# A Hyena layer's filters made beside the product in front of it, and its convolutions laid among its input panels

## The reference

```python
def hyena_mixer(h, w_in, short_w, short_b, f_w1, ..., f_skip, w_out):
    v, x1, x2 = jnp.split(depthwise_conv3(h @ w_in, short_w, short_b), 3, axis=-1)
    h_freq = hyena_filters(seq, f_w1, f_b1, f_w2, f_b2, f_w3, f_freq)   # hid @ w3, decayed, / sum |h|, rfft
    def long_conv(u, n):
        uf = u.astype(jnp.float32)
        y = jnp.fft.irfft(jnp.fft.rfft(uf, n=2 * seq, axis=1) * h_freq[:, n], n=2 * seq, axis=1)[:, :seq]
        return (y + uf * f_skip[n].astype(jnp.float32)).astype(u.dtype)
    z = x1 * long_conv(v, 0)
    z = x2 * long_conv(z, 1)
    return z @ w_out
```

## Time and profile before

| | |
|---|---|
| median of 3 runs | 1804.94 us |
| profiled execution, its own time | 1802.81 us |
| its span | 1801.0 us |
| TensorE busy | 1740.6 us (97%) |
| VectorE busy | 1230.6 us (68%) |
| ScalarE busy | 985.2 us (55%) |

### The profile page before, as it was taken

How to read it: one execution, slowest core, us unless ns; L and a number is a source line. 1 busy time by engine, 2 the same in 40 slices (tenths; PEclk the granted TensorE clock), 3 DMA queues, 4 the chain that set the end, 5 groups by cost and what they waited for, 6 DMA issues and landing times.

```text
span 1801.0 us, 37562 instructions
## 1 busy us (share of the span) xinstructions
PE 1740.6 (97%) x13784; PEld 1646.0 (91%) x13784; DVE 1230.6 (68%) x2017; ACT 985.2 (55%) x1368; POOL 12.8 (1%) x20
## 2 busy tenths in 40 slices
PE   7999999999999998999999999999999999999997
PEld 7999999888999987569999999999999777799997
DVE  6887666586666587888666678766566656576654
ACT  4467744365775444216774446775454644467742
POOL 0000200000000000000000000000000000000000
PEclk9999999999999999999999999999999999999999
DMA  6567564433656453205666456656455332256661
GB/s 208 170 197 228 185 219 141 150 105 106 198 183 217 157 198 127 82 1 156 194 184 217 138 175 178 197 186 236 158 174 152 127 132 69 71 174 188 185 214 67
DMA packets 79400, 290.13 MB, mean 161 GB/s; under 512 B 9723, under 2 KB 12124, under 8 KB 79196
## 3 DMA queue, kind: packets, MB, share of 16 engines
q1 hardware_dynamic: 79324, 289.12, 50.6%
HBM read 288.03 MB, written 1.05 MB: 161 GB/s over the span
## 4 chain that ended last, share of the span: by engine, by line
PE 86%; DVE 9%; issue 2%; ACT 2%; DMA 1%; DVEq 0%; SPq 0%; ACTq 0%
PE bank L490 24%; PE bank L492 24%; PE bank L491 24%; DVE wlo L1440 2%; PE bank L802 2%; PE bank L781 1%; PE bank L721 1%; DVE conv_cv L1548 1%; DVE rinv L1446 1%; PE bank L865 1%; PE bank L963 1%; PE bank L700 1%; PE bank L973 0%; DMA raw<-in_w 0%; PE bank L936 0%
## 5 line engine op out<-in xcount | busy, mean ns | idle before, releaser
L490 PE MATMUL bank<-xh,whi 128*128 128x256 f32 (+1 forms) x2736 | 775.5, 283 | 11.0 <-DVE wlo L1440 10.6
L491 PE MATMUL bank<-xl,whi 128*128 128x256 f32 (+1 forms) x2736 | 772.1, 282 | 0.0
L492 PE MATMUL bank<-xh,wlo 128*128 128x256 f32 (+1 forms) x2736 | 771.4, 282 | 0.0
L1060 ACT CAST whi<-raw 128x1024 fp32r<-128x1024 f32 (+1 forms) x490 | 538.3, 1099 | 367.6 <-PE bank L492 322.6
L1440 DVE TENSOR_TENSOR wlo<-raw,whi 128x1024 fp32r<-128x1024 f32 (+1 forms) x491 | 629.1, 1281 | 4.8 <-ACT whi L1060 2.7
L490 PEld LDWEIGHTS bank<-xh,whi 128*128 128x128 f32 x2736 | 518.6, 190 | 26.8 <-issue 15.3
L492 PEld LDWEIGHTS bank<-xh,wlo 128*128 128x128 f32 x2736 | 519.2, 190 | 0.0
L491 PEld LDWEIGHTS bank<-xl,whi 128*128 128x128 f32 x2736 | 515.9, 189 | 0.1
L490 PE MATMUL bank<-ffn_hh,whi 128*128 128x256 f32 x880 | 246.7, 280 | 0.0
L492 PE MATMUL bank<-ffn_hh,wlo 128*128 128x256 f32 x880 | 246.7, 280 | 0.0
L491 PE MATMUL bank<-ffn_hl,whi 128*128 128x256 f32 x880 | 245.7, 279 | 0.0
(11 more groups left out here) (323 smaller groups left out, 2034.2 us busy)
## 6 DMA issues: line engine op xcount, KB each, us to landing
raw<-in_w SPq DMA_DIRECT2D x414, 512.0 KB, 3.6
raw<-in_w SPq DMA_DIRECT2D x80, 704.0 KB, 4.2
att_bias<-in_bias SPq DMA_DIRECT2D x4, 512.0 KB, 5.3
hy_w<-in_filt_w SPq DMA_DIRECT2D x8, 256.0 KB, 4.3
hy_decay<-in_decay SPq DMA_DIRECT2D x4, 512.0 KB, 5.2
mla_uq<-in_uq SPq DMA_DIRECT2D x1, 1152.0 KB, 5.2
x<-in_xT SPq DMA_DIRECT2D x1, 1024.0 KB, 5.8
out<-x SPq DMA_DIRECT2D x8, 128.0 KB, 2.0
```

The source lines that it names most:

```text
L490: pe.matmul(ps, whi[:, slot, wc], hi[:, k, cols], start=first, stop=False)
L491: pe.matmul(ps, whi[:, slot, wc], lo[:, k, cols], start=False, stop=False)
L492: mm = pe.matmul(ps, wlo[:, slot, wc], hi[:, k, cols], start=False, stop=last)
L1060: nc.scalar.copy(whi[:, p % RING, 0:k * P], raw[:, p % RING, 0:k * P]).then_inc(panel_hi, 1)
```

## The change

- The filter sets 0 and 1 are made beside the 16 panels of `down1`, the product in front of the Hyena layer (`first_filters`, one list of steps per engine, called after each panel). Their tables are loaded among the panels of `up1`, to buffers laid behind the feed-forward's.
- The 24 panels of `in2` are written out one by one; from panel 8 on they take turns in two banks, 0 and 1. Filter sets 2 and 3 use banks 2 and 3, the convolutions banks 4 to 7.
- Units 0, 1 and 2 are laid among the panels, one per six panels: TensorE does `turn` after panel 5+6u, `spectra` after 6+6u and 7+6u, `back` after 9+6u and 10+6u; VectorE does `multiply` behind its steps for panels 7+6u and 8+6u, `unit_out` behind 10+6u and 11+6u. Unit 3 stays behind the panels, with the rest of set 3.
- The skip terms are made by ScalarE (`skip`), not by VectorE. The copy that mended the first row of the magnitudes is replaced by a memset before the maximum.
- The key's rotation moves behind gate panel 12; the first sigmoid moves behind the first query of the latent attention.

The diff, cut to what the text speaks of:

```diff
-    hyx = overlay("hyx", [("ab", [P, 2, 2, HC], F32), ("ut", [P, 2, HC], F32), ("am", [P, 2, HC], F32)])
+    hyx = overlay("hyx", [("ut", [P, 2, HC], F32)])
+    skipped = [up[:, 0, 0:SEQ], up[:, 1, 0:SEQ], square[:, 0, 0:SEQ], square[:, 1, 0:SEQ]]
+    def in2_bank(p):
+        return (IN2.b0 + (p if p < 8 else p % 2)) % 4
 # SP
+            elif name == "up1":
+                panels(ph, 0, 8)
+                sp.wait_ge(y_lo, YBASE["in1"] + C)
+                sp.dma_start(hy["hdft"][:], a["hdft"]).then_inc(hs["tables"], 16)
+                panels(ph, 8, 4)
+                filter_inputs(0)
+                panels(ph, 12, 4)
+                sp.dma_start(hy["idft"][:], a["idft"]).then_inc(hs["tables"], 16)
...
+            elif name == "down1":
+                panels(ph, 0, 9)
+                more_filter_inputs(1)
+                panels(ph, 9, 7)
             elif name == "in2":
-                panels(ph, 0, 8)
-                sp.wait_ge(panel_used, ph.p0)
-                sp.dma_start(hy["fdft"][:], a["fdft"]).then_inc(hs["tables"], 16)
...
-                filter_inputs(0)
-                panels(ph, 8, 16)
+                panels(ph, 0, 3)
+                more_filter_inputs(2)
+                panels(ph, 3, 16)
+                more_filter_inputs(3)
+                panels(ph, 19, 5)
 # TensorE, beside down1
+        def first_filters(p):
+            if p in (0, 7):
+                for r in range(2):
+                    filters(p // 7, r)
+            elif p in (4, 11):
+                pe.wait_ge(hs["tables"], 64)
+                filter_sums(p // 7)
+                filter_spectra(p // 7, range(3))
+            elif p in (5, 12):
+                filter_spectra(p // 7, range(3, 5))
 # TensorE, in2
+            for p in range(2, 24):
+                if p < 8:
+                    panel(ph, 0, p, xh, xl, A, None)
+                else:
+                    panel(ph, 0, p, xh, xl, A, None, (in2_bank(p), ph.t0 + p + (1 if p < 10 else 3)))
+                u, at_ = divmod(p - 5, 6)
+                if p == 14:
+                    filter_sums(2)
+                    filter_spectra(2, (0,))
+                elif p == 15:
+                    filter_spectra(2, (1, 2))
+                elif p == 17:
+                    filter_spectra(2, (3, 4))
+                if 0 <= u < 3:
+                    if at_ == 0:
+                        turn(u)
+                    elif at_ in (1, 2):
+                        spectra(u, at_ - 1)
+                    elif at_ in (4, 5):
+                        back(u, (2 * at_ - 8, 2 * at_ - 7))
+                if p in (8, 10):
+                    filters(2, (p - 8) // 2)
+                elif p in (19, 21):
+                    filters(3, (p - 19) // 2)
+            turn(3)
+            filter_sums(3)
+            filter_spectra(3, (0,))
+            spectra(3, 0)
+            filter_spectra(3, (1, 2))
+            spectra(3, 1)
+            filter_spectra(3, (3, 4))
+            out_slices(range(0, HJ))
+            back(3, range(HJ))
             out_slices(range(HJ, C))
 # TensorE: what the new steps wait for
+            def turn(u):
...
+                if u < 2:
+                    pe.wait_ge(hs["zin"], HJ * (u + 1))
+                if u:
+                    pe.wait_ge(hs["z"], HJ * (u - 1) + 2)
...
+            def back(u, js):
+                pe.wait_ge(hs["Y"], 2 * u + 2)
 # ScalarE
+            def skip(u):
...
+                for j in range(HJ):
+                    cc = HJ * (u % 2) + j
+                    e = nc.scalar.activation(skipped[j], hy["z"][:, cc, :], ACT.Identity, bias=0.0,
+                                             scale=v("c_skip", u // 2 * C + cc))
+                e.then_inc(hs["skip"], 1)
+            for p in range(24):
+                tap(0, p, K8)
+                if p in (5, 11, 17, 23):
...
+                    turned((p - 5) // 6)
+                if p in (8, 14, 20):
...
+                    skip((p - 8) // 6)
...
 # VectorE, in2
+            for p in range(24):
+                conv_step(p)
+                u, at_ = divmod(p - 7, 6)
+                if p == 6:
+                    wing_weights(2)
+                elif p == 9:
+                    decayed(2, 0)
+                elif p == 11:
+                    decayed(2, 1)
+                elif p == 13:
+                    filter_magnitudes(2)
+                elif p == 14:
+                    inverse_sum(2)
+                elif p == 16:
+                    wing(2, 0)
+                if 0 <= u < 3:
+                    if at_ in (0, 1):
+                        multiply(u, at_)
+                    elif at_ == 3:
+                        unit_out(u, (0, 1))
+                    elif at_ == 4 and u < 2:
+                        unit_out(u, (2, 3))
...
+                elif p == 23:
+                    filter_magnitudes(3)
+                    unit_out(2, (2, 3))
+            inverse_sum(3)
+            wing(3, 0)
+            wing(3, 1)
+            multiply(3, 0)
+            multiply(3, 1)
+            unit_out(3, range(HJ))
-                if g == 2:
-                    key_rope()
...
             gate_tile(12)
+            key_rope()
             gate_tile(13)
```

More of the change, by code:

```diff
@@ L683, in attention @@
                 panel(PH["out1"], j // 4, j % 4, at["yh"], at["yl"], A, None)
-        def hyena(norm):
[L686 to L722, removed]
-            def turn(u):
[L726 to L729, removed]
@@ new lines, in filters @@
+        def filters(n, r):
+            pe.wait_ge(hs["ws"], n + 1)
+            if r and n >= 2:
+                pe.wait_ge(hs["ab"], 2 * n + 1)
+            elif n == 2:
+                pe.wait_ge(bank_free, IN2.t0 + 12)
+            elif n and not r:
+                pe.wait_ge(hs["wings"], n)
+                pe.wait_ge(hs["middle"], n)
+                pe.wait_ge(hs["inv"], n)
+            for part in range(2):
+                rows = slice(FHID * part, FHID * part + FHID)
+                mm = pe.matmul(filter_bank(n, part, r)[:], filt_hid[rows, r * P:(r + 1) * P], pair[rows, :],
+                               start=True, stop=True)
+            mm.then_inc(hs["F"], 1)
@@ L736, in out_slices @@
+            def back(u, js):
+                pe.wait_ge(hs["Y"], 2 * u + 2)
+                for j in js:
+                    for i in range(4):
+                        mm = pe.matmul(bank[4 + j][:, 0:SEQ], hy["frY"][:, i, j * P:(j + 1) * P], hy["idft"][:, i, :],
+                                       start=i == 0, stop=i == 3)
+                    mm.then_inc(hs["back"], 1)
             def out_slices(ks):
@@ L752, in out_slices @@
                             mm.then_inc(panel_used, 1)
-            ph = PH["in2"]
+            ph = IN2
             first_panels(ph, xh, xl, A, (x_lo, C * norm), norm, A)
[L756 to L791, removed]
-                else:
[L793 to L804, removed]
@@ L1007, in _ @@
             norm += 1
-            product(f"down{layer}", ffn["hh"], ffn["hl"], A, (hid_lo, FC * layer))
+            if layer == 1:
+                for p in range(16):
+                    panel(PH["down1"], p // 4, p % 4, ffn["hh"], ffn["hl"], A, (hid_lo, FC))
+                    first_filters(p)
+            else:
+                product(f"down{layer}", ffn["hh"], ffn["hl"], A, (hid_lo, FC * layer))
         retention_in(norm)
@@ L1085, in step @@
                 split_hi(ph, 0, i, j, k)
-            steps(act, ph, 0, ph.n, step, loop=gain is not None)
+            if between is None:
+                steps(act, ph, 0, ph.n, step, loop=gain is not None)
+            else:
+                for p in range(ph.n):
+                    step(p // 4, p % 4, ph.k if p + 4 < ph.n else ph.next_k)
+                    between(p)
         def conv_tap(name, m):
@@ L1481, in step @@
                                     square[:, (j // 2 if half else j) % 2, next_cols], ALU.add).then_inc(sum_added, 1)
-            dve_steps(ph, 0, ph.n, step)
+            if between is None:
+                dve_steps(ph, 0, ph.n, step)
+            else:
+                for p in range(ph.n):
+                    step(p // 4, p % 4, ph.k if p + 3 < ph.n else ph.next_k)
+                    between(p)
         def scaled(ph, first, n, dst, keep=None):
```

380 lines of the change are left out of this document (215 added, 165 removed).

## The result

The changed kernel took 1820.16 us in the median of 4 runs (1816.5 to 1824.04), the kernel before 1804.93 beside it (1802.77 to 1805.02): a ratio of 1.0085, 95% interval 1.007 to 1.01. It is slower by 15.2 us, where 9.7 were forecast; the time lies just above the forecast's own range (1809 to 1820) and inside the range for 8 in 10. The profiled execution took 1818.93 us (span 1817.1), 16.1 more of span than before.

What follows compares the result with a forecast made beforehand. TensorE, 86% of the chain, was taken to bound the kernel, through its waits and lower clock. Waits 8.2, clock 4.8, down product 0.6, latent part -3.9: +9.7 us on 1802.81, 1812.5, as median 1814.6; 8-in-10 range 1801.5 to 1821.

Steps and rivals of the forecast that it cites:

- VectorE's order: Hyena stage: TensorE waits for VectorE's in-order steps; waits 20.5 us after against 12.3 before, +8.2.
- The 0.7 for the first turned values: Hyena, after panel 6: a wait of 0.7 us (0 to 1), since VectorE starts the stage late.
- totals right, order wrong: Rival: VectorE runs ahead at panels 7 and 19, multiplies are ready in time; -5.4 us, 1799.5; chance 0.15.
- The clock inside Hyena: Lower clock behind Hyena's waits: 11.8 us lost against 7.0 before, +4.8 (bounds of the loss none and 15.3).
- Filter sets moved: Two filter sets lengthen the down product by 16.2 us and shorten Hyena by 16.2: zero.
- the ledger: The forecast's sum of waits and work walked in queue order, with a falling clock: +9.7 us; chance 0.67.
- The page's estimate: Hyena's clock loss by the skill page: eight waits at 0.83, 6.7 us in place of 11.8.
- The down product: Feed-forward in front of Hyena: 16.2 us longer by the moved sets, plus one added wait of 0.6.
- Under 1 us: none: Clock rule: waits shorter than 1 us were taken to cost no lower clock.
- The latent part: Latent attention: key wait of 3.0 and 1.7 of low clock go, 0.8 comes back; -3.9 us (-4.7 to -1.5).
- The rival of late transfers: Table transfers or filter inputs make one weight panel late: 6.5 us more, 1821; chance 0.06.
- Skips: Hyena: skip terms moved from VectorE to ScalarE cost zero (0 to 1 us).

Runs made afterwards that it cites:

- the earlier multiplies: Changed kernel with each multiply of units 0 to 2 one panel earlier in VectorE's order: 1806.5 us, ratio 1.0011 to the kernel before.
- the earlier tail: On top of the earlier multiplies, the last filter set made 1 to 3 panels earlier: 1796.29 us, ratio 0.995 to the kernel before.
- The filled waits: Changed kernel with idle matmuls put where TensorE waits, VectorE's order unchanged: 1812.76 us, ratio 1.004 to the kernel before.
- The last experiment: On top of the earlier tail, set 0's sums one panel later in the down product, first sigmoid back in its old place: 1792.47 us, ratio 0.9925.
- The kernel with the latent edits alone: Kernel before with only the key rotation behind gate panel 12 and the first sigmoid behind the first query: 1803.64 us, ratio 0.9992.
- skips on VectorE: Changed kernel with the skip terms made by VectorE again: 1823.62 us, ratio 1.0102 to the kernel before.
- changed again: The changed kernel itself, unaltered, run again as reference: 1819.54 us, ratio 1.008 to the kernel before.
- tables: Kernel before with only the Hyena tables and first filter inputs loaded among the up panels: 1803.55 us, ratio 0.999.

## Why the prediction was right, and where not

**Right in sign and in VectorE's order, 5.5 us short in size; three terms were off and partly cancelled.** By step:

- **VectorE's order.** 3.6, 0.8, 2.0, 3.6, 3.2, 0.3 and 6.3 were predicted; 3.51, 1.21, 1.96, 3.88, 3.65, 0.76 (the L818 line) and 6.27 measured. The 0.7 for the first turned values isn't there. In total 21.2 against 20.5. That the cause is the order and not the load is shown: the earlier multiplies take away the three waits at equal work, the earlier tail the two behind panel 23. The rival "totals right, order wrong" needed VectorE to be 3.6 us ahead at panel 7; it was not, as it can't evict a panel before that panel is done.
- **The clock inside Hyena.** 11.8 us predicted, 2.9 + 1.7 + 1.7 + 2.9 = 9.2 measured: behind 3.51 us of waiting 2.9, behind 3.88 1.7, behind 3.65 and the sums 1.7, behind 1.96 nothing, behind 6.27 2.9. The kernel before had lost 7.5 by its trace, not 7.0, so the clock adds 1.7 to the stage and not 4.8. The filled waits show that three of the four falls follow the idle time: with matmuls there, they are gone.
- **Filter sets moved: "zero" was wrong.** The prediction let 16.2 us leave Hyena and the same 16.2 arrive in the down product. By the traces the work at full speed falls by 14.4 in the Hyena stage and grows by 17.1 in the down product, 2.6 us more in all. Much of this is in the panels: summed from start to start, without what the clock and the waits cost, the same 575 panel and output matmuls in Hyena take 72.8 us in 20 groups, 69.0 in 6 before, and those behind 560 us in the down product and the first panels of in2 70.3 in 9 groups, 68.8 in 3. So each return from inserted steps to a panel costs about a quarter of a microsecond, by this estimate.
- **Hyena as a whole: near by luck.** The stage is 3.7 us shorter, where the ledger had 3.2 (the 16.2 moved out, less 8.2 and 4.8). The waits were 0.8 and the work 1.8 worse than it said, the clock 3.1 better.
- **The page's estimate.** The estimate from the Trainium skill, page "TensorE: Matmul & The Clock Gate", section "HAM oscillation — how this bites in real kernels", was 6.7 us. The trace agrees that waits bring a throttled clock. Its size per wait doesn't hold here: each stretch cost 1.7 or 2.9 us of work, and three of Hyena's seven waits cost none, for 9.2 in all, midway between the two estimates.
- **The down product: the term mis-sized.** 16.2 + 0.6 was predicted, 19.3 measured: 17.1 of work (above), the wait of 0.76, and the lower clock behind it, 1.7 us; a wait in front of in2's panel 3 is 0.2 shorter. "Under 1 us: none" is the rule that failed here: the one-column matmuls of the sums stand behind that wait. The last experiment, which removes the wait, finds the clock at 1.00.
- **The latent part: the gain is there, and is given back.** Up to the rotated query the changed kernel gains 3.9 us, exactly the ledger's figure. Then the clock falls behind the query's wait, which is 3.0 and was 2.3 (1.7 us), and again, by 3.1, behind mrg_yl's, a wait of 2.41 us against 2.42 before, in work that the change doesn't touch. Before, neither was followed by a fall. These 4.8 us are most of the 6.4 by which the span (+16.1) exceeds the forecast, and this is the step that failed: waits that the edit leaves as they are, or nearly, were taken to cost what they had cost. The kernel with the latent edits alone gains 3.5 in its stretch, and what its span lacks was lost ahead of the edit.
- **Transfers.** "Nothing late" held: no DMA wait in in2, and between 442 and 567 us TensorE is busy 124.2 us in both kernels. The rival of late transfers is out.
- **Skips.** They were costed at zero (0 to 1); with them on ScalarE the waits are 0.7 us shorter, and the times don't resolve more.

In the span the points add up: 3.1 beyond the sets in the down product, +12.5 in Hyena (16.2 less 3.7), -3.9 in the latent part, +1.7 and +3.1 behind it: 16.5, against 16.1. One reading of the prediction was wrong without harm: 1.92 us is the price of a set's filters, not of one half; its sum of 8.09 a set uses it rightly.

**What stays open.** Why the same wait of 2.4 us for mrg_yl is followed by no fall (before, earlier multiplies, latent alone, skips on VectorE, tail and down), by a stretch of 3.4 us (filled) or of 6.8 (changed, changed again, tables, tail). The work around it is the same in all. I found nothing in the work around the wait that tells them apart; whether the moment in time at which it lies decides was not tested. It may be why runs of one kernel differ by 1.4 to 10 us; that was not shown. Neither was the cost of a return to the panels tested by an edit of its own. Not tried: four banks for in2's panels in place of two.

## What to carry over

When work of several engines is interleaved by hand, averages (108 us against 122.6) say nothing; walk each queue from the last point where both engines meet, and put a producer's step ahead of the periodic step that nobody waits for yet. Here six calls, moved by one panel, were worth 13 us. Work that is moved between busy stages isn't free either: here it came back 2.6 us dearer. Price a removed wait with the clock behind it, but hold against it that a fall further on may come or go by luck: a gain of one or two falls (1.7 to 3.4 us) can't be promised from one profile, and needs many runs to be seen.

## What I had not expected of the hardware

- A fall can follow a wait under 1 us. Behind 0.76 us and the 16 one-column matmuls of the sums in the down product, behind 0.21 us and the 16 sums in the filled kernel, and behind 1.07 us and the sums in the kernel with the earlier tail, the clock was at its lower level for 3.4 us. But it need not: behind 0.74 us and the same 16 sums in the kernel with the early tables (693.67) no fall came. What part the narrow matmuls have in it was not tested.
- A fall can stand where TensorE has not waited. At about 347 us, in work that is the same in all kernels, six of the ten profiles have a stretch of 3.4 us behind four matmuls of two columns and eight with 16 rows, with no wait above 0.15 us in the 20 us ahead; the other four, the kernel before among them, run on at 1.00.
- A wait does not fix what its fall costs. The query's wait of 3.0 us is followed by a fall of 3.4 us in the changed kernel and by none in the one with the latent edits alone; at 2.3 us, by none in the kernel before and by one of 3.4 in the fastest kernel (at 1483.2).
